# Two-block transformer forward in fp32: the conv branch's gate projection is computed beside the neighbourhood attention's jobs, and the order of the first merge is changed

## The reference, cut to what matters

```python
(a_glu, a_gate, nq, nk, nv, n_gate, wq, wk, wv, w_gate, merge) = jnp.split(h @ w_in[l], SPLIT_POINTS, axis=-1)

def conv_branch(u_glu, u_gate, conv_w, conv_b, ln_g, ln_b, w_proj):
    a = u_glu[..., :D_CONV] * jax.nn.sigmoid(u_glu[..., D_CONV:])
    a = depthwise_conv(a, conv_w, conv_b)             # 31 taps, 512 channels
    a = jax.nn.silu(layer_norm_2(a, ln_g, ln_b))
    return (a * jax.nn.silu(u_gate)) @ w_proj
...
y_a = conv_branch(a_glu, a_gate, ...)
y_b = (o_na * jax.nn.silu(n_gate)) @ w_proj_b
y_c = (o_wa * jax.nn.silu(w_gate)) @ w_proj_c
y = sigmoid(g_a) * y_a + sigmoid(g_b) * y_b + sigmoid(g_c) * y_c      # g_a, g_b, g_c: the merge gates
return y @ w_o
```

## Time and profile before

| | us |
|---|---|
| median of 3 runs | 4013.05 (4012.01 to 4015.1) |
| the profiled execution, its own time | 4022.73 |
| span of its profile | 4021.5 |
| PE, DVE, ACT, POOL busy | 3736.0, 2216.7, 1490.8, 1071.2 |
| layer 0's jobs begin, layer 0's first conv projection begins | 2516.4, 2704.8 |
| layer 1's jobs begin, layer 1's first conv projection begins | 3493.6, 3607.5 |

### The profile page before, as it was taken

The page is one execution under the profiler, slowest core; times in us unless marked ns, Lnnn a source line. Parts: engine busy times, 40 slices in busy tenths (PEclk is TensorE's granted clock), DMA queues, the critical chain, the costliest instruction groups (busy, mean ns, idle before and its releaser), DMA issues.

```text
span 4021.5 us, 53026 instructions
## 1 busy us (share of the span) xinstructions
PE 3736.0 (93%) x20868; PEld 3101.4 (77%) x20868; DVE 2216.7 (55%) x3743; ACT 1490.8 (37%) x2554; POOL 1071.2 (27%) x715
## 2 busy tenths in 40 slices
PE   5999999989999999898999889799999989899999
PEld 4888868778888888747988867578877867678777
DVE  6555784576667777745532579831156237841452
ACT  3223553444225323444422423342235224353352
POOL 1102104232014201303201422843211333354224
PEclk8999999989999999998999999799999999899999
DMA  7565324235654555303332411111110112112112
GB/s 269 170 203 166 131 69 157 94 131 183 224 179 154 188 185 167 118 37 108 130 95 89 132 37 53 48 35 66 53 48 12 63 53 74 63 48 92 66 35 92
DMA packets 131590, 433.90 MB, mean 108 GB/s; under 512 B 14480, under 2 KB 14608, under 8 KB 130704
## 3 DMA queue, kind: packets, MB, share of 16 engines
q1 hardware_dynamic: 130912, 427.89, 31.6%
q10 hardware_dynamic: 432, 2.62, 0.2%
HBM read 428.36 MB, written 2.10 MB: 107 GB/s over the span
## 4 chain that ended last, share of the span: by engine, by line
PE 76%; DVE 13%; ACT 4%; issue 3%; DMA 2%; POOL 1%; SPq 0%; DVEq 0%; ACTq 0%; POOLq 0%
PE ps L618 22%; PE ps L619 21%; PE ps L620 21%; DVE cut L2164 4%; PE ps L1858 1%; DVE cut L544 1%; PE ps L1735 1%; ACT cut L534 1%; PE ps L616 1%; PE ps L645 1%; PE ps L1819 1%; PE ps L646 1%; PE ps L647 1%; ACT cut L1884 1%; PE ps L1835 1%
## 5 line engine op out<-in xcount | busy, mean ns | idle before, releaser
L618 PE MATMUL ps<-cut 128*128 128x512 f32 (+1 forms) x5344 | 1909.8, 357 | 164.7 <-DVE cut L544 42.5
L619 PE MATMUL ps<-cut 128*128 128x512 f32 (+1 forms) x5344 | 1875.3, 351 | 0.0
L620 PE MATMUL ps<-cut 128*128 128x512 f32 (+1 forms) x5344 | 1873.4, 351 | 0.0
L618 PEld LDWEIGHTS ps<-cut 128*128 128x128 f32 x5344 | 1033.1, 193 | 337.2 <-issue 85.5
L619 PEld LDWEIGHTS ps<-cut 128*128 128x128 f32 x5344 | 1034.3, 194 | 131.8 <-issue 5.3
L620 PEld LDWEIGHTS ps<-cut 128*128 128x128 f32 x5344 | 1032.9, 193 | 129.3
L544 POOL TENSOR_TENSOR cut<-cut 128x1024 fp32r<-128x1024 f32 (+3 forms) x280 | 605.4, 2165 | 1221.8 <-ACT cut L534 1221.4
L534 ACT ACTIVATE cut<-cut 128x1024 fp32r<-128x1024 f32 (+3 forms) x680 | 632.3, 938 | 793.3 <-PE ps L620 698.1
L544 DVE TENSOR_TENSOR cut<-cut 128x1024 fp32r<-128x1024 f32 (+3 forms) x400 | 480.8, 1205 | 445.4 <-ACT cut L534 445.1
L875 POOL TENSOR_TENSOR cut<-cut 128x512 fp32r<-128x512 f32 (+1 forms) x100 | 147.2, 1472 | 1047.5 <-ACT cut L836 1047.4
L2164 DVE SCALAR_TENSOR_TENSOR cut<-cut,cols 128x512 f32<-128x512 f32 (+1 forms) x330 | 280.1, 849 | 11.7
(11 more groups left out here) (297 smaller groups left out, 3506.5 us busy)
## 6 DMA issues: line engine op xcount, KB each, us to landing
cut<-in_ffn_in SPq DMA_DIRECT2D x200, 512.0 KB, 3.6
cut<-in_mod_w SPq DMA_DIRECT2D x128, 512.0 KB, 4.1
cut<-in_ffn_out SPq DMA_DIRECT2D x96, 384.0 KB, 3.2
cut<-in_ffn_out SPq DMA_DIRECT2D x96, 320.0 KB, 3.0
cut<-in_w_ada SPq DMA_DIRECT2D x48, 512.0 KB, 3.3
cut<-in_w_merge SPq DMA_DIRECT2D x48, 512.0 KB, 3.3
cut<-in_even_in SPq DMA_DIRECT2D x36, 512.0 KB, 3.4
cut<-in_proj SPq DMA_DIRECT2D x48, 256.0 KB, 2.6
```

What stands on the lines that cost most here:

```text
L618: te.matmul(o, hi[:, k - ka, w], xs[0], start=k == 0, stop=False)
L619: te.matmul(o, hi[:, k - ka, w], xs[1], start=False, stop=False)
L620: ins = te.matmul(o, lo[:, k - ka, w], xs[0], start=False, stop=last)
```

## The change

The gate's matmuls run beside the attention's jobs, at the steps that `GATE_STEPS` gives. In layer 0 each m is in two pieces, first the context's 256 columns (group 1) and two steps later the 512 (group 0): steps 3, 5, 7, ..., 17. In layer 1 each m is one piece, at steps 3, 6, 9, 12. ACT copies the raw sums into buffers that are dead by then (`SG`: the keys of the first heads and the values' scratch), and applies the Silu to them later, in `act_conv_norm`, between the root and the conv's own Silus. The gate's low parts are made by DVE in place of POOL. Merge gate 0 runs at the step behind the last job's scores, merge gate 1 between means and squares, and merge gate 2 and all the rest behind the squares. ACT, too, empties merge gates 0 and 1 there. The conv's scratch for the context moves within `t512`, since the Sigmoids of the merge gates are written earlier.

```diff
+GATE_TILES = (2, 3, 0, 1)
+GATE_STEPS = [{3 + 4 * m + 2 * i: (m, (1 - i,)) for m in range(4) for i in range(2)}, {3 + 3 * m: (m, (0,)) for m in range(4)}]
...
-            lin((gate, l), "w2_" + gate, (l,), range(4), low="g")
+            lin((gate, l), "w2_" + gate, (l,), range(4) if i else GATE_TILES, low="g" if i else "v")
...
-    SG = region(P1 + 6144, 4, 768)
+    SG = [ar(o, o + 768) for o in (P1 + 3072, P1 + 3840, Z0 + 7680, Z0 + 8448)]
...
-            if not gis or 0 in gis:
-                ins.then_inc(*sig("p_mm", name, m))
+            ins.then_inc(*sig("p_mm" if not gis or 0 in gis else "p_mm1", name, m))
...
-        return t512[(8 if h0 else 0) + i][:, 0:n]
+        return t512[(4 if h0 else 0) + i][:, 0:n]
...
+        se.wait_ge(*(yield "a_agc", l, 3, 0))
+        for t in range(4):
+            x = SG[t][:, 0:groups_of(l)[-1][1]]
+            se.activation(x, x, ACT.Silu).then_inc(*sig("a_ag", l, t))
...
         yield from pe_pairs(("na", l), na_jobs(l), at_step({
-            0: lambda: nv(3), 1: lambda: values(2), 2: lambda: values(3), n: lambda: agate(0), n + 1: lambda: agate(1)}))
+            0: lambda: nv(3), 1: lambda: values(2), 2: lambda: values(3), n: lambda: amerge(MERGES[:1]),
+            **{s: lambda p=p: agate(*p) for s, p in GATE_STEPS[l].items()}}))
         yield from pe_conv_means(l)
-        yield from agate(2)
+        yield from amerge(MERGES[1:2])
         yield from pe_conv_squares(l)
-        yield from agate(3)
-        yield from pe_merge(l, 0, QG, lambda k, gi: [(("v_bl0", "g_bl0")[k % 2], l, k)])
+        yield from amerge(MERGES[2:])
...
-            0: lambda: nv(3), 1: lambda: values(2), 2: lambda: values(3), 5: lambda: act_slabs(LIN["agate", l].ahead(0))}))
-        yield from agate(0, 1)
+            0: lambda: nv(3), 1: lambda: values(2), 2: lambda: values(3),
+            **{s: lambda p=p: agate(*p) for s, p in GATE_STEPS[l].items()}}))
+        yield from act_merge(l, 0, QG, MERGES[:1])
         yield from act_conv_squares(l)
-        yield from agate(2)
-        yield from agate(3)
-        yield from act_slabs(LIN["merge", l, 0, 0].ahead(0))
+        yield from act_merge(l, 0, QG, MERGES[1:2])
         yield from act_conv_norm(l)
...
+        yield from low_slabs("v", ve, LIN["nv", l].ahead(2))
         yield from dve_head_scale(("nk", l), NK, GR, gq[:, 1:2])
...
+        def na_beside(i):
+            if i == 1:
+                yield from low_slabs("v", ve, LIN["nv", l].ahead(3))
+            if i in GATE_STEPS[l]:
+                yield from low_slabs("v", ve, LIN["agate", l].ahead(GATE_STEPS[l][i][0]))
+            yield from dve_taps(l, 2)
```

More of the change, by code:

```diff
@@ L261 @@
     "a_mla": ("a_cq", "a_qn", "a_qp", "a_kn", "a_vm", "a_trig"),
[L262 removed]
+    "a_heads": ("a_agc", "a_nq", "a_nk", "a_nk0", "a_vt0", "a_vt", "a_nv", "a_wq", "a_wk", "a_wv", "a_ag"),
     "a_conv": ("a_cm", "a_cs2", "a_glu"),
@@ L2407, in pe_second, with agate, amerge @@
         yield from pe_head_sums(("nk", l), GR, 6)
-        def agate(m):
-            return pe_linear(("agate", l), nrhs, QG, lambda m, gi: ("a_ag", l, m, gi), none, ms=[m])
+        def agate(m, gis):
+            return pe_linear(("agate", l), nrhs, QG, lambda m, gi: ("a_agc", l, m, gi), none, ms=[m], gis=gis)
+        def amerge(items):
+            return pe_merge(l, 0, QG, lambda k, gi: [(("v_bl0", "g_bl0")[k % 2], l, k)], items)
         yield from nv(2)
@@ L2524, in act_second, with agate, epilogue @@
         yield from values(1)
-        def agate(*ms):
-            return act_linear(("agate", l), to(SG, ("agate", l), "a_ag", QG, ACT.Silu), ms)
+        def agate(m, gis):
+            def epilogue(m):
+                for gi in gis:
+                    c0, c1 = QG[gi]
+                    se.wait_ge(*(yield "p_mm1" if gi else "p_mm", ("agate", l), m))
+                    se.activation(SG[GATE_TILES[m]][:, c0:c1], PS[bank[("agate", l), m, gi]][:, 0:c1 - c0], ACT.Copy).then_inc(*sig("a_agc", l, m, gi))
+            return act_linear(("agate", l), epilogue, [m])
         n = len(na_jobs(l))
         yield from act_pairs(("na", l), na_jobs(l), at_step({
-            0: lambda: nv(3), 1: lambda: values(2), 2: lambda: values(3), 5: lambda: act_slabs(LIN["agate", l].ahead(0))}))
-        yield from agate(0, 1)
+            0: lambda: nv(3), 1: lambda: values(2), 2: lambda: values(3),
+            **{s: lambda p=p: agate(*p) for s, p in GATE_STEPS[l].items()}}))
+        yield from act_merge(l, 0, QG, MERGES[:1])
         yield from act_conv_squares(l)
-        yield from agate(2)
-        yield from agate(3)
-        yield from act_slabs(LIN["merge", l, 0, 0].ahead(0))
+        yield from act_merge(l, 0, QG, MERGES[1:2])
         yield from act_conv_norm(l)
@@ L2541, in act_second @@
         se.wait_ge(*(yield "g_bl0", l, 3))
-        yield from act_merge(l, 0, QG)
+        yield from act_merge(l, 0, QG, MERGES[2:])
         se.wait_ge(*(yield "p_mm", ("proj", l, 0, 7), 0))
@@ L2611, in dve_second @@
         ve.wait_ge(*(yield "p_hb", ("nk", l), 3, 1))
-        yield from dve_pairs(("na", l), na_jobs(l), lambda i: dve_taps(l, 2))
+        def na_beside(i):
[4 more added lines that the diff above has]
+            yield from dve_taps(l, 2)
+        yield from dve_pairs(("na", l), na_jobs(l), na_beside)
         yield from dve_taps(l, 99)
@@ L2618, in dve_second @@
             if t == 0:
-                ve.wait_ge(*(yield "a_ag", l, 3, len(QG) - 1))
+                ve.wait_ge(*(yield "a_ag", l, 3))
             if t == 2:
@@ L2623, in dve_second @@
                 ve.wait_ge(*(yield "g_bl0", l, 1))
-            ve.tensor_tensor(f, AG[:, t, 0:nq], SG[:, t, 0:nq], ALU.mult).then_inc(*sig("v_b0", l, t))
+            ve.tensor_tensor(f, AG[:, t, 0:nq], SG[t][:, 0:nq], ALU.mult).then_inc(*sig("v_b0", l, t))
             if t % 2 == 0:
```

## The result

The changed kernel takes 4034.3 us (median; 4032.0 to 4039.0) against 4014.1 us (4012.0 to 4021.6) for the kernel before in the same session. The ratio is 1.0046, with a 95% interval of 1.0034 to 1.0059: slower by about 20 us. The prediction said 4032.5 and gave slower 0.82.

The account below looks back on a forecast made before the run. PE, busy 93% of the span, was taken as the bound, with the chain from the conv's squares to the first projection deciding. Layer 0's +11.2 and layer 1's +9.6 gave +20.8 us, shaded by 1.3 to 4032.5; range 4018 to 4043.

Parts of the forecast that it names:

- The stall, +14.0 and +8.1: Before projection 0, PE idles 17.2 us (layer 0) and 12.9 (layer 1), against 3.2 and 4.8; S ends the squares' matmuls.
- The four Silus at no cost: Layer 0, ACT: the raw gates' extra Silus, 3.5 us, fit a 3.9 us gap before the first conv Silu.
- the means' wait of -2.3: Layer 0: the means no longer wait 2.3 us for ACT to empty gate 1.
- projection 0's low of 1.3: Behind the last split POOL needs 1.26 us for projection 0's low half, its high half being early.
- the signs in the jobs: Layer 0's jobs end at least 15 us later, else the forecast is wrong; layer 1's jobs lengthen by 22 us.
- The low halves on DVE, +7.4: Layer 0's jobs: gate lows moved from POOL add DVE work and waits for ACT's highs; +7.4 us, bounds +4 to +11.
- The 5.55 us piece at step 5, +4: Layer 0's jobs: the 512-column gate piece overfills PE's step and makes PE late; +4 us, bounds 0 to +8.
- The lift of the clock, -2: Layer 0's jobs: steadier PE work raises the clock and repairs the slow stretch behind step 7; -2 us, 0 to -3.
- POOL's taps, 0: POOL's taps no longer wait for ACT's gate highs and end earlier, but the means come after the jobs anyhow; 0.
- A: Rival: layer 0's gates are swallowed in PE's free time beside the jobs, so faster, down to 4001 us; chance 0.05.
- B: Rival: a wash at 4013 us, with stalls of some 10 and 7 us and all low halves hidden; chance 0.13.
- C: Rival: worse, 4045 at most: ACT held at gate steps, 512 piece at half clock, Silus not fitting their gap; chance 0.06.

Follow-up runs that it names:

- k1: The changed kernel with the last of four gate groups (tile 1) put back behind the squares in each layer; 4015.9 us, ratio 1.0007 to the kernel before.
- k2: The changed kernel with the last two gate groups (tiles 0 and 1) put back behind the squares; 3996.1 us, ratio 0.9956 to the kernel before.
- dvelate: The changed kernel with DVE making its low halves for the gates one step later in the jobs; 4031.9 us, ratio 1.0038 to the kernel before.
- hold: The changed kernel with POOL's taps made to wait for ACT's high half of the second gate slab; 4034.4 us, ratio 1.0050 to the kernel before.

## Why the prediction was right, and where its terms were off

**The stall, +14.0 and +8.1.** Right. It named Sqrt at S + 2.0 (measured 1.9) and projection 0 at S + 25.5 (25.3) in layer 0 and S + 18.3 (18.3) in layer 1, so stalls of 17.2 and 12.9 us: 16.9 and 12.6 were measured, +13.7 and +7.8. k1 and k2 show that they are on the path. The four Silus at no cost, the means' wait of -2.3 and projection 0's low of 1.3 held too. So did the signs in the jobs: from the first to the last score matmul they are 30.8 us longer in layer 0 (at least 15 were asked for) and 22.4 in layer 1 (22).

By the drain of the Trainium skill (ScalarE: Activation LUTs, What ACT_TABLE_LOAD costs) Sqrt would have started 1.4 us later in each layer; the trace gives 0.02 us behind the load.

**The low halves on DVE, +7.4.** The steps with them are 1.1 (step 1), 3.3 and 2.9 us longer, with 0.4 in the step behind the last, less 0.9 at step 0, where POOL's low no longer disturbs: +6.8. The wait was 1.88 us in place of 2.0. dvelate shows that it lay on the path.

**The 5.55 us piece at step 5, +4.** Mis-sized: it delayed DVE by nothing. DVE's steps 4, 5 and 6 take 7.75, 7.99 and 7.97 us, in the kernel before 7.71, 7.98 and 7.95. The argument added the piece to PE's average work of a step and took the excess over the step as a delay. It left out the slack around the piece: PE had waited 5.6 us for DVE just ahead of that step, ran the piece from 2542.8 to 2550.6 (7.8 us, at a clock of 0.71), did two more steps' scores and waited for DVE again, 1.9 us, until 2557.3.

**The lift of the clock, -2.** It didn't come. The stretches of the kernel before, to be laid beside those of after under dvelate (to the end of step 7, the next 7.5 us, the rest up to the means):

```profile
2509.90:2580.50 70.60, 49.88 (x293) 36.60 (x292) 62.98 (x160) 18.87 (x52) 52.96 (x58) 0.74 0.11 38
2580.50:2588.00 7.50, 7.50 (x62) 5.80 (x60) 5.26 (x23) 5.39 (x15) 6.76 (x10) 0.67 0.37 140
2588.00:2648.80 60.80, 58.51 (x563) 46.78 (x559) 33.65 (x143) 27.51 (x83) 49.10 (x58) 1.00 0.08 27
```

Up to the end of step 7 the clock rose, 0.74 to 0.81, but DVE is the bound there: the stretch grew by 6.9 us, the lows' share, and the three pieces are hidden. PE's idle time in it didn't shrink, as the prediction's sign had it, but went from 20.7 to 22.6 us: for pieces of 11.2 us at full clock PE was busy only 5.0 us longer, since its clock rose. The slow stretch behind it stayed, 0.67 before and 0.69 after, since PE had stood 5.9 us for DVE's step 7; the 0.96 of the second window of after, above, is this stretch, and behind it both kernels run at 1.00. Layer 0's jobs stage grew by 20.2 us; the moved groups (three more, 25.0) less the hidden 11.2, the lows' 6.8, less the means' 2.3, and 0.3 for the pipeline's last jobs make 18.6. Of the 1.6 us left, 1.1 is step 9's piece of 512 columns, which runs in the slow stretch and took 6.65 us (2579.44 to 2586.09) in place of 5.55. So +4 - 2 were forecast for the two terms and at most +1.6 came, and the one error partly covers the other: luck.

**POOL's taps, 0.** Wrong. The prediction saw that they start earlier and asked only when they end. They start at 3451.0 in place of 3501.1 in layer 1 and run beside DVE's taps in the heads. The stage from layer 0's last heads to layer 1's first job grew by 4.2 us, and hold gives 2.9 of it back. The Trainium skill (SBUF — State Buffer, Who interferes with whom) says that a VectorE instruction with two inputs in SBUF contends with a GpSimd instruction that reads SBUF, and that the shared ports are an exclusive lock. The traces agree, and show the blocking one by one. A tap of 512 columns, 0.75 us alone, that starts inside one of POOL's low halves (after, layer 1's heads):

```profile
3439.94 2.67 POOL L549 TENSOR_TENSOR cut<-cut 128x1024 fp32r<-128x1024 f32 x1 [10.10 <-ACT cut L539]
3440.40 2.77 DVE L2168 SCALAR_TENSOR_TENSOR cut<-cut,cols 128x512 f32<-128x512 f32 x1
```

It ends 0.55 us behind POOL's instruction. POOL's taps are shorter (1.03 and 0.79 us on average there, 0.93 and 0.73 in the kernel before), so they cost DVE less each: 0.65 in place of 0.52 us for a tap. By the page this would have been a term of the sum.

**Layer 1.** Its jobs grew by 16.9 us (three groups more, 16.4, and +0.5 where +1.3 stood in the sum), and the stage behind the means shrank by 9.3 us where 16.35 - 7.8 - 0.2 = 8.4 were due.

**The sum.** +20.8 predicted, +20.6 in the stages, +20.2 in the medians. The stages of the two layers grew by 9.5 and 7.6 us where 11.2 and 9.6 were forecast (the stalls and the lows 0.6 us under each, layer 1's jobs 0.8, the piece and the lift 0.4; the rest, in the two stages behind the means, isn't placed), and the 4.2 us ahead of layer 1's jobs, which weren't in the sum, make up for it. So the total is better than its parts, by luck. The shading by 1.3 us had no ground in a row and moved the forecast away from the result.

**The rivals.** A needed the gates swallowed after step 7: DVE's taps do end there, and layer 0's pieces at steps 9 to 17 took their full time. B needed stalls of 10 and 7 us. C's costs didn't appear: the Silus found their gap, PE's waits for ACT in layer 0's jobs are 1.6 us at most, and the 512 piece, though it ran in part at half clock, delayed nothing. C's own sum was also off: 20.8 + 4 + 4 + 7 on 4013 is 4049, not 4045.

## What to carry to other kernels

Work that covers a chain of other engines is worth more where it stands than its own duration says: before moving it, measure the chain from its first link to the consumer, and move only what exceeds it. Here two of four groups could go, and 38 us lay between moving two and moving four. Where a chain has already outrun its cover, look first at which in-order engine starts it late; one reordered Sqrt gave 12 us without moving any matmul. And an engine relieved of work starts its next work earlier: ask what that next work will run beside.

## What the hardware showed that was not expected

A tap of DVE that starts inside a low half of POOL doesn't end before POOL's instruction does. In after there are 23 taps of 512 columns that overlap one by 0.3 us or more, and each ends 0.55 us behind POOL's end, whenever it started; every other trace has 22 to 24 of them, with the same 0.55 us. Beside POOL's taps DVE's of 256 columns take 0.65 us in place of 0.52 (11 in 7.18 and 5.70 us). Through the taps a mere shift of POOL's work moved a wait of PE by 4.0 us.

The two starts of layer 0's first job (2499 to 2503 and 2507 to 2510 us) may have their like in the times: in the session of k1, seven of the kernel before lie at 4010 to 4013 us and seven at 4016 to 4020. What sets the one or the other no run here explains.
